# Second feed-forward product: seven-product form for ten of eleven weight tile pairs, in two passes, with weight sums made by adding transfers

## The reference, cut to what matters

```
def swiglu_ffn(x, g, w_in, w_out):
    h = rmsnorm(x, g)
    gate, up = jnp.split(h @ w_in, 2, axis=-1)        # 1024 -> 2 x 2816
    return x + (jax.nn.silu(gate) * up) @ w_out       # 2816 -> 1024
...
    return rmsnorm(x, g_final)
```

## Time and profile before

| | us |
|---|---|
| median of 3 runs | 900.63 (900.3 to 900.65) |
| the profiled execution | 900.4 |
| its span in the trace | 898.7 |
| TensorE matmuls busy | 888.4 |
| VectorE busy | 596.2 |
| ScalarE busy | 385.7 |
| mean rate of the transfers | 120 GB/s |

### The profile page before, as it was taken

How to read it: one execution, slowest core, us unless ns; L and a number is a source line. 1 busy time by engine, 2 the same in 40 slices (tenths; PEclk the granted TensorE clock), 3 DMA queues, 4 the chain that set the end, 5 groups by cost and what they waited for, 6 DMA issues and landing times.

```text
span 898.7 us, 13165 instructions
## 1 busy us (share of the span) xinstructions
PE 888.4 (99%) x5292; PEld 793.1 (88%) x5292; DVE 596.2 (66%) x711; ACT 385.7 (43%) x555; POOL 57.5 (6%) x59
## 2 busy tenths in 40 slices
PE   9999999999999999999999999999999999999997
PEld 7998888889999998988888888899999999888886
DVE  5685666789577678755466476998888887433333
ACT  5654432345444444523244332554555445322223
POOL 0111000000000000024100053000000000000000
PEclk9999999999999999999999999999999999999999
DMA  9946332213322222672211122222322233322212
GB/s 350 364 168 265 110 105 94 94 47 99 137 93 95 94 100 89 226 289 94 92 49 51 44 94 107 81 95 97 127 103 93 93 116 117 117 93 94 94 48 94
DMA packets 16091, 108.17 MB, mean 120 GB/s; under 512 B 1840, under 2 KB 1968, under 8 KB 4016
## 3 DMA queue, kind: packets, MB, share of 16 engines
q1 hardware_dynamic: 13408, 93.99, 28.3%
q10 hardware_dynamic: 2176, 12.00, 3.5%
q0 software_dynamic: 464, 1.57, 0.5%
HBM read 101.26 MB, written 6.29 MB: 120 GB/s over the span
## 4 chain that ended last, share of the span: by engine, by line
PE 84%; DVE 10%; ACT 4%; issue 2%; DMA 1%; SPq 0%; POOLq 0%; POOL 0%; ACTq 0%; DVEq 0%
PE psum L1445 28%; PE psum L1447 27%; PE psum L1446 27%; DVE blk L870 2%; ACT blk L395 1%; DVE sig L1155 1%; DMA pack<-first 1%; DVE tl L870 1%; DVE wl L870 1%; DVE raw L1061 1%; DVE raw L1059 1%; DVE raw L1060 1%; DVE merged L1158 0%; ACT wh L395 0%; PE psum L1697 0%
## 5 line engine op out<-in xcount | busy, mean ns | idle before, releaser
L1445 PE MATMUL psum<-th,w7h 128*128 128x256 f32 x504 | 142.7, 283 | 0.3 <-ACT snap L395 0.3
L1447 PE MATMUL psum<-th,w7l 128*128 128x256 f32 x504 | 142.6, 283 | 0.0
L1446 PE MATMUL psum<-tl,w7h 128*128 128x256 f32 x504 | 142.6, 283 | 0.0
L870 DVE TENSOR_TENSOR wl<-raw,wh 128x2048 fp32r<-128x2048 f32 (+1 forms) x44 | 89.4, 2043 | 50.0 <-ACT wh L395 49.9
L1445 PEld LDWEIGHTS psum<-th,w7h 128*128 128x128 f32 x504 | 96.8, 192 | 0.6 <-issue 0.5
L1446 PEld LDWEIGHTS psum<-tl,w7h 128*128 128x128 f32 x504 | 96.8, 192 | 0.0
L1447 PEld LDWEIGHTS psum<-th,w7l 128*128 128x128 f32 x504 | 96.8, 192 | 0.0
L395 ACT ACTIVATE wh<-raw 128x2048 fp32r<-128x2048 f32 (+1 forms) x44 | 73.1, 1675 | 20.8 <-PE psum L1447 19.5
L1445 PE MATMUL psum<-hh,wh 128*128 128x512 f32 x192 | 75.0, 391 | 0.0
L1447 PE MATMUL psum<-hh,wl 128*128 128x512 f32 x192 | 74.7, 389 | 0.0
L1446 PE MATMUL psum<-hl,wh 128*128 128x512 f32 x192 | 74.7, 389 | 0.0
(11 more groups left out here) (265 smaller groups left out, 2197.3 us busy)
## 6 DMA issues: line engine op xcount, KB each, us to landing
raw<-weights SPq DMA_DIRECT2D x79, 1024.0 KB, 4.8
pack<-first SPq DMA_DIRECT2D x3, 768.0 KB, 7.9
vraw<-weights SPq DMA_DIRECT2D x2, 1024.0 KB, 12.1
xt<-xt SPq DMA_DIRECT2D x1, 2048.0 KB, 18.7
X<-x SPq DMA_DIRECT2D x2, 1024.0 KB, 27.7
X<-x ACTq DMA_DIRECT2D x1, 2048.0 KB, 10.1
memt<-memt SPq DMA_DIRECT2D x1, 1024.0 KB, 22.6
kv_store<-kh ACTq DMA_DIRECT2D x1, 1024.0 KB, 3.9
```

The lines of the kernel that those rows point to most:

```text
L870: return V.tensor_tensor(dst, v, f32(hi), ALU.subtract)
L1445: nc.tensor.matmul(dst, lh, rh, start=start, stop=False, **kw)
L1446: nc.tensor.matmul(dst, lh, rl, start=False, stop=False, **kw)
L1447: return nc.tensor.matmul(dst, ll, rh, start=False, stop=stop, **kw)
```

## The change

Ten of the eleven pairs get the seven-product form; the pair (two tiles of 128 rows) is the depth, the two halves of the 512 tokens and the two halves of the 1024 output columns are the other block dimensions. All seven partial products, each of 256 tokens by 512 columns (two banks), do not fit in the eight banks together with the sums, so the pairs are gone through twice: in the first pass three products each (P1, P5, P6, 18 matmuls), in the second four (P2, P3, P4, P7, 24 matmuls). Between and during the passes ScalarE keeps P1, P5 and the sum of P1 and P6 in SBUF (`kept`), the residual is transposed into six tiles `xres` in between, and VectorE merges at the end; the eleventh pair is added plainly, 48 matmuls, into the merged banks.

```diff
+            for i in range(NP):
+                p, last = i % SLOTS, i == NP - 1
...
+                out_product(4, p, 0, 2, start=i == 0, signal=done)
+                pe.wait_ge(hsl_ready, i + 1)
+                pe.wait_ge(lo_ready, FO0 + i + 1)
+                out_product(6, p, 2, 0, start=i == 0, signal=done)
+                if i == 0:
+                    pe.wait_ge(hid_ready, HT - 1)
+                out_product(0, p, 1, 1, start=i == 0, signal=done, closing=True).then_inc(panel_done, 1)
```

```diff
+            for q in range(2 * NP + 1):
+                if q < 2:
+                    sp.wait_ge(lo_ready, FO0 + q - 1)
+                elif q < 4:
+                    sp.wait_ge(panel_done, FO0)
+                else:
+                    sp.wait_ge(lo_ready, FO0 + q - 3)
+                dst = fo_raw(q)
+                if q < NP:
+                    src, dst = fo_in[q, :, 0:3 * S], dst[:, 0:3 * S]
+                elif q < 2 * NP:
+                    src = fo_in[q - NP, :, 2 * S:6 * S]
...
+            def first_sum(q):
+                pool.wait_ge(*fo_landed(q, 1))
+                if q < NP:
+                    dst, src = fo_raw(q)[:, 0:S], fo_in[q, :, 3 * S:4 * S]
+                else:
+                    dst, src = fo_raw(q)[:, 0:2 * S], fo_in[q - NP, :, 5 * S:7 * S]
+                pool.dma_start(dst, src, accum_op=ALU.add).then_inc(fo_sum[q % 4], 16)
+            def second_sum(q):
+                pool.wait_ge(*fo_landed(q, 2))
+                w = fo_raw(q)
+                dst, src = (w[:, S:2 * S], w[:, 0:S]) if q < NP else (w[:, 0:S], w[:, S:2 * S])
+                pool.dma_start(dst, src, accum_op=ALU.add).then_inc(fo_sum[q % 4], 16)
+            first_sum(0)
+            for q in range(1, 2 * NP):
+                first_sum(q)
+                second_sum(q - 1)
```

ScalarE and VectorE split each pair in two steps, first what needs no sum, then the sums:

```diff
+            def first_pass_hi(i):
+                p = i % SLOTS
+                act.wait_ge(hid_ready, 2 * i + 2)
+                act.wait_ge(panel_done, FO0 + i - 1)
+                copy(hsh[p][:, 0, 0:Q], hid[:, 2 * i, 0:Q]).then_inc(hid_first_hi, 1)
+                act.wait_ge(*fo_landed(i, 1))
+                copy(foh[p][:, 2 * S:3 * S], fo_raw(i)[:, 2 * S:3 * S]).then_inc(fo_first_hi, 1)
+            def first_pass_sums_hi(i):
+                p = i % SLOTS
+                act.wait_ge(token_sums, i + 5)
+                copy(flat(hsh[p])[:, Q:Q + S], hid[:, 2 * i, :]).then_inc(hsh_ready, 1)
+                act.wait_ge(*fo_landed(i, 3))
+                copy(foh[p][:, 0:2 * S], fo_raw(i)[:, 0:2 * S]).then_inc(hi_ready, 1)
...
-            act_window(NS - 1, 1, None, more=False, early=(lambda: fo_weights_hi(0), lambda: fo_hid_hi(0)))
+            act_window(NS - 1, 1, None, more=False, early=(lambda: first_pass_hi(0), lambda: first_pass_sums_hi(0)))
```

`second_pass_hi`, `second_pass_rest_hi`, `first_pass_lo` and `second_pass_lo` are built alike. Several semaphores are renamed or shared. In the gate stage two lines of VectorE's loop change places:

```diff
                 merge(h - 1, 2)
+                gate_prep(n + 1, i + 1)
                 merge(h - 1, 3)
-                gate_prep(n + 1, i + 1)
                 gate_prep_lo(n + 1, i + 1)
```

More of the change, by code:

```diff
@@ L69 @@
 FO0 = FI0 + HT
-PANELS = FO0 + HT // 2
+NP = 10
+FB0 = FO0 + NP
+FC0 = FB0 + NP
+PANELS = FC0 + 1
 C_MEM, C_MIX, C_X, C_FFN = 0, 8, 16, 24
@@ new lines, in keep_part @@
+            def keep_part(which, product, src):
+                for m in range(2):
+                    act.wait_ge(*part_done(product, m))
+                    copy(kept[:, which, m, :], bank[src + m]).then_inc(fo_kept, 1)
+            act_window(NS - 1, 1, None, more=False, early=(lambda: first_pass_hi(0), lambda: first_pass_sums_hi(0)))
+            strassen_silu(1, NS - 1)
+            for i in range(1, NP):
+                first_pass_hi(i)
+                first_pass_sums_hi(i)
+                if 3 <= i < 9:
+                    keep_residual(i - 3)
@@ new lines, in _ @@
+            second_pass_hi(0)
+            second_pass_rest_hi(0)
+            keep_part(0, "P1", 4)
+            for i in range(1, NP):
+                if i == 1:
+                    act.wait_ge(panel_done, FB0 + i - 1)
+                second_pass_hi(i)
+                if i == 1:
+                    keep_part(1, "P5", 6)
+                    for m in range(2):
+                        act.wait_ge(fo_merged, m + 1)
+                        copy(kept[:, 2, m, :], bank[m]).then_inc(fo_kept, 1)
+                second_pass_rest_hi(i)
@@ new lines, in merge_part @@
+            def merge_part(b, product, which, m, kept_by=0):
+                dve.wait_ge(*part_done(product, m))
+                if kept_by:
+                    dve.wait_ge(fo_kept, kept_by)
+                src = kept[:, which, m, :] if which is not None else xres[:, m, :]
+                if product == "P7":
+                    V.tensor_tensor(bank[b], src, bank[b], ALU.subtract).then_inc(fo_merged, 1)
+                else:
+                    V.tensor_tensor(bank[b], bank[b], src, ALU.subtract if product == "P3" else ALU.add).then_inc(fo_merged, 1)
@@ new lines, in out_product @@
+            def out_product(banks, p, a, w, start=False, signal=None, free=None, closing=False):
+                h, g = hsh[p][:].rearrange("p a b -> p (a b)"), hsl[p][:].rearrange("p a b -> p (a b)")
+                c = slice(w * S, (w + 1) * S)
+                for m in range(2):
+                    if free:
+                        pe.wait_ge(free[0], free[1] + m)
+                    r = slice(a * Q + m * P, a * Q + (m + 1) * P)
+                    ins = mm3(bank[banks + m], h[:, r], g[:, r], foh[p][:, c], fol[p][:, c], start, signal is not None, skip_group_check=True)
+                    if signal and not (m == 1 and closing):
+                        ins.then_inc(signal, 1)
+                return ins
```

326 lines of the change are left out of this document (216 added, 110 removed).

## The result

The changed kernel takes **924.2 us** (median of 4 runs, 922.5 to 925.9) against 900.6 (900.3 to 900.65): a ratio of 1.026 with a 95% interval of 1.025 to 1.028. The forecast was 893.5 us and its range ended at 909. The change makes the kernel 23.6 us slower, where 7 us faster had been expected.

What follows compares the result with a forecast made beforehand. TensorE's matmuls were taken as the bound. Span: 898.7 - 13.6 - 1.6 + 6.0 + 0.6 + 0.8 + 0.2 + 0.7 = 891.8 us; with 1.7 us more, 893.5 us, range 888 to 909.

Steps and rivals of the forecast that it cites:

- price of the adding transfer: Second feed-forward product: each adding transfer costs near a plain one, landing after 3.5 us.
- rival 1: Second feed-forward product: adding transfers read twice, DMA engines become the bound; 905 us (897 to 910), chance 0.25.
- Gate stage: Preparing the next panel ahead of the last merge removes three 0.5 us waits on the gsnap copy: -1.6 us.
- Hold in the last gate/up panel: ScalarE's high part of the first pair's sums delays a copy that TensorE's last product needs: +0.6 us.
- Matmuls: Second feed-forward product: 468 matmuls instead of 528, 60 fewer at 0.2267 us each: -13.6 us.
- Turn: From first to second pass, TensorE waits for VectorE's work on pair 0's second operands: +0.8 us (0 to 3).
- eleventh pair: Before the last pair, VectorE's low parts follow two merges, 5.6 us against 5.44: +0.2 us.
- First gap: Start of the second product: pair 1's second sum stands behind load 2's landing, so TensorE waits: +6.0 us.
- Hardly one after it: Sign of a right forecast: after one TensorE gap of 5 to 8 us in the second product, hardly another.
- no queue of chained transfers keeps the 16 engines full: Said while pricing rival 1's DMA work of 109 us; at 90% it would be 12 us more.
- Clock: After the new idle in the second product, matmuls may run at the lower clock: +0.7 us (0 to +2.5).
- rival 3: Adding transfers slower still, or GpSimd takes several us to issue one: over 915 us, chance 0.10.

Runs made afterwards that it cites:

- kernel with plain copies: The changed kernel with every adding transfer made a plain copy of the same size, queue, waits and order, so the weight sums are missing: 898.5 us (one run).
- early sums: The changed kernel with all weight sums made in memory ahead of the last stage, which has one plain load per pair: 887.96 us on both chips.
- kernel with one exchange: The changed kernel with pair 1's second sum issued on GpSimd ahead of pair 2's first sum: 923.3 us, ratio 1.0239.
- kernel with 32 columns: The changed kernel with every adding transfer cut to 32 columns instead of 512 or 1024, same order and waits: 893.65 us (one run).

## Why the prediction was wrong

**The step that failed** is the price of the adding transfer: "I take it near the plain row, landing after 3.5 us, because the row of the same size, queue and kind of rows in SBUF is the nearest one". The nearest row by form was a plain transfer, and it says nothing of what an addition does. The price is 2.0 to 2.1 times plain by bytes, above the 1.5 from which rival 1 decides, and at or just above the 2 at which I had put its end. Already the first adding transfer, alone in 751 to 757 us, shows it: 256 KB at 32.4% of 6 us, 1.9 us of the 16 engines. The same transfer as a plain copy (750.5 to 756.5 us of the kernel with plain copies) takes 0.9.

```profile
q0 software_dynamic: 144, 0.26, 32.4%
```

```profile
q0 software_dynamic: 80, 0.26, 15.1%
```

The argument against rival 1, that the second addend lies in SBUF and single slices reach 415 GB/s, was none: the additions from SBUF to SBUF came out as the dearer kind, if only by a tenth. The Trainium skill (Collectives: The Full Stack, section The bandwidth ceiling: the fold count and why AG ≠ RS ≠ AR) says of the reducing step of a collective that its add needs two source reads and so runs at half rate; the measured 2.0 to 2.1 agrees, for ordinary transfers of one core. I had quoted that rule with 0.25 beside it and no row that spoke against it.

**The sum, term by term**, in the span (predicted 891.8, measured 924.1):

- *Gate stage* -1.6: right in kind, 2.3 us when measured alone. I had taken the listed waits without what they cost at their edges.
- *Hold in the last gate/up panel* +0.6: 2.3 us. The mechanism was right: ScalarE's high part of the sums (766.68) stands ahead of the `snap` copy (767.65). The second sum of pair 0 took 4.9 us to land, not 2.9, beside the first sum of pair 1. With plain copies it is 0.6.
- *Matmuls* -13.6: right. With the sums out of the way the stage is 12.1 us shorter; the rest is 0.4 us of waits and about 1 us that I cannot place.
- *Turn* +0.8 and *eleventh pair* +0.2: TensorE has no wait in either place in the changed kernel. With early sums the turn has one of 0.2 us and the eleventh pair none.
- *First gap* +6.0: 8.0, in the predicted place. The chain of waits of the changed kernel, piece by piece:

```profile
769.86 4.45 DMA more<-fo
...
774.59 0.54 POOL more L429
775.13 5.63 DMA raw<-raw
...
780.79 1.06 ACT foh L451
...
781.88 1.24 DVE fol L976
```

The load took 4.45 us (4.1 estimated), GpSimd 0.54, the second sum 5.63 (3.5), the two splits 2.3. All pieces are those named; the mis-sized one is the adding transfer. But it was not the only chain with that gap: the kernel with one exchange shows that pair 2's own sums make one of nearly the same length.

- *"Hardly one after it"*: wrong. Nine more waits, 18.6 us in all, of 0.4 to 5.0 us, from 803 to 891 us. They follow from the full DMA engines. I had also written that no queue of chained transfers keeps the 16 engines full; these did, to 99%.
- *Clock* +0.7: about 7 us. I had one idle in mind (the one of the first gap); there are four places with some 35 slow matmuls, 0.2 us each. The last of them begins 1.3 us after the end of a wait of only 2.0 us.

From 769.66 to the last matmul's end at 918.2 the stage takes 148.5 us, 37.2 more than the 111.3 of the kernel with early sums: 26.6 of waits, 7 of slow matmuls, and 3.6 us more. Some 2.5 of these stand at the edges of the ten waits: the last matmul ahead of a wait is listed with 0.39 us where the next one would start after 0.23, and the first one behind it is about 0.1 us slower. The other 1 us stays unplaced.

**The rivals.** Rival 1 was what happened, and the signs given for it are there: engines full from 770 to 890 us, adding transfers that mostly land after 6.8 to 9.3 us (medians of the groups on the page; 4.4 and 5.2 for the 256 KB ones from memory), high and low parts that wait for the sums. The wait of a microsecond in every pair of the second pass came in six of ten, with 0.4 to 2.2 us. Its price of 905 (to 910) was too low. It had 109 us of work for the engines from time 0 to the last sum; measured, that sum is issued at 894.0 and split by ScalarE at 898.6, 129 us after time 0 (769.8), and in this time the engines work 124 us. Both figures have the last load in them. GpSimd's queue takes 73.7 us of it where some 63 were counted, SyncE's loads 50.4 where 46 were: an added byte costs 5.9 us per MB and not twice the 2.6 of the earlier trace rows, a plain one beside others 2.8. The second sum of pair 1, which also falls into this time, had been left out. From that split to the last matmul it is 19.6 us, where 15.9 were counted.

Against the plain price of the earlier trace rows, from which the prediction reckoned, an added byte costs 2.3 times, and the time of 924 lies where rival 3 was priced (over 915). Of the other half of rival 3, several microseconds for an issue, nothing came: an adding transfer is listed with 0.87 to 1.23 us on GpSimd (0.60 in the earlier trace rows), and the next one can start 0.54 after it. The kernel with 32 columns, which has all these issues, shows that this costs next to nothing here.

## What to carry to other kernels

A transfer that adds has to be priced as one that moves twice its bytes or a little more (2.0 to 2.1 times here); where its bytes, counted twice, and the plain loads together ask more engine time than the stage has, the DMA engines become the bound, as 1.75 and 2.5 MB a pair did here. Sums of weights that depend on no result of the kernel can be made where the transfers are idle, even with extra copies, and loaded plainly where time is short. And where no row shows a new operation, its form is a poor guide: ask what it has to read, and give the dear end the larger chance unless a row excludes it.

## What the runs showed of the hardware

- An adding transfer costs the DMA engines 5.87 us per MB, a plain one 2.82 to 2.90 (from q0's shares above). From SBUF to SBUF it is about 2.1 times plain, from memory about 1.9; at half the width 6.5 us per MB beside other transfers. The first adding transfer, alone, takes 1.94 us of the engines at full width and 0.96 at half, so there the width makes no difference per byte.
- GpSimd is listed with 0.87 us for issuing an adding transfer, and with up to 1.23 where one is issued right behind another, against 0.54 for the same transfer as a plain copy. The next issue starts 0.54 us after the one before in both kernels.
- After idles of 4.5 to 8 us in the changed kernel TensorE is granted 1.2 GHz for the next 8 to 10 matmuls, starts 0.43 us apart, and then 2.4 GHz again; in the kernel with one exchange 6 to 11 matmuls are slow after idles of 3.6 to 5.8 us. Idles of 0.4 to 2.3 us passed without it in seven places of the changed kernel. After four others, of 2.0 us there and of 2.4, 2.5 and 3.0 us in the kernel with one exchange, TensorE first worked at 2.4 GHz again for 0.6 to 1.8 us, and only then 6 or 7 matmuls were slow. What tells these cases apart is open. The Trainium skill (TensorE: Matmul & The Clock Gate, section What's actually happening) says that the slow state is the default and activity releases it; the return after 6 to 11 matmuls agrees.
- In the kernel with the sums made early the trace ends 4.8 us after the last store is issued on ScalarE's queue, in the kernel before 3.0. The stores of that queue land 2.5 us after their issue in both (median of four); what fills the rest is not shown.
